# First mixer's attention tiles between the parts of the mLSTM heads, a norm per head, and the second mixer's probabilities in PSUM

## The reference

```python
# first block
h = rms_norm(x, g); z = h @ w_in
y_a = mlstm_group(q_m, k_m, v_m, o_m, gates, ...)   # 4 heads, both directions, 4 chunks of 128
y_b = mla_group(c_q, c_kv, k_pe, ...)               # 4 heads: softmax(q k^T) v over 512 keys
x = x + concat(y_a, y_b) @ w_out
h = rms_norm(x, g); x = x + square(relu(h @ w_ff1)) @ w_ff2
# second block
ret_out = silu(rg) * rmsnorm(retention(rq, rk, rv))
a = softmax(s0) - lam * softmax(s1)                 # causal, 4 heads
diff_out = rmsnorm(a @ v, g)
x = x + concat(ret_out, diff_out) @ w_out
x = x + peer(rmsnorm(x, g), ...)                    # 16 of 128 keys per half query, 16 of 256 pairs
out = rmsnorm(x, g)
# inside mlstm_group
h = rms_norm(h_fw + h_bw, g_out)                    # per head of 128 columns
return sigmoid(o) * h
```

## Time and profile before

| | |
|---|---|
| median of 3 runs | 2564.78 us (2561.06 to 2567.64) |
| profiled execution | 2563.88 us, its span 2562.1 us |
| busy in the span | PE 94%, DVE 52%, ACT 31%, POOL 33% |
| first mixer, four mLSTM heads | 164.9 to 261.2 us |
| first mixer, 16 attention tiles | 261.3 to 327.6 us |
| second mixer, differential tiles | about 815 to 932 us |
| wait for the last key selection | 1139.9 to 1150.0 us |

### The profile page before, as it was taken

How to read it: one execution, slowest core, us unless ns; L and a number is a source line. 1 busy time by engine, 2 the same in 40 slices (tenths; PEclk the granted TensorE clock), 3 DMA queues, 4 the chain that set the end, 5 groups by cost and what they waited for, 6 DMA issues and landing times.

```text
span 2562.1 us, 29145 instructions
## 1 busy us (share of the span) xinstructions
PE 2404.5 (94%) x11589; PEld 1209.4 (47%) x11797; DVE 1329.6 (52%) x2379; ACT 805.9 (31%) x880; POOL 847.1 (33%) x221
## 2 busy tenths in 40 slices
PE   7987889999989888889999999999999999999998
PEld 3456445444444454444466544444444444444443
DVE  2654526454532542689999555555555552222223
ACT  3221324333332333211189532222222232323222
POOL 0000215555553144531000253333333333424231
PEclk9985899999999999999999999999999999999999
DMA  5010035988863105763467986666666657666531
GB/s 202 33 66 1 1 148 164 246 246 244 247 191 105 66 34 169 215 176 119 160 273 303 345 241 188 184 182 185 184 186 180 182 176 201 170 174 180 138 91 41
DMA packets 401649, 424.98 MB, mean 166 GB/s; under 512 B 275578, under 2 KB 342270, under 8 KB 388740
## 3 DMA queue, kind: packets, MB, share of 16 engines
q1 hardware_dynamic: 395204, 411.93, 53.2%
q10 hardware_dynamic: 6336, 11.54, 1.2%
HBM read 283.97 MB, written 72.35 MB: 139 GB/s over the span
## 4 chain that ended last, share of the span: by engine, by line
PE 74%; DVE 17%; ACT 4%; DMA 2%; issue 2%; POOL 1%; DVEq 0%; SPq 0%; POOLq 0%; ACTq 0%
PE ps L1490 43%; PE ps L1765 14%; DVE arena L2428 5%; DVE arena L2435 4%; PE ps L1803 2%; DMA gate_matrix<-split 2%; PE ps L1303 2%; ACT split L1224 2%; PE ps L1588 1%; ACT arena L1210 1%; PE ps L1301 1%; PE ps L1276 1%; PE ps L1781 1%; PE ps L1432 1%; PE ps L1782 1%
## 5 line engine op out<-in xcount | busy, mean ns | idle before, releaser
L1490 PE MATMUL ps<-split,arena 128*128 128x512 bf16 x4232 | 936.6, 380 | 22.8 <-DVE x_sb L2450 9.0
L1490 PEld LDWEIGHTS ps<-split,arena 128*128 128x128 bf16 x4320 | 421.2, 98 | 534.1 <-DVE x_sb L2450 14.4
L852 POOL TENSOR_TENSOR split<-ring,split 128x4096 bf16<-128x4096 f32 x32 | 259.3, 8103 | 892.1 <-ACT split L1224 892.1
L1765 PE MATMUL ps<-arena 128*128 128x512 bf16 x1881 | 415.4, 379 | 2.1
L2450 DVE TENSOR_TENSOR x_sb<-ps,x_sb 128x512 f32<-128x512 f32 x256 | 173.8, 689 | 323.2 <-PE ps L1490 323.2
L759 POOL TENSOR_TENSOR split<-ring,split 128x4096 bf16<-128x4096 f32 x27 | 215.2, 7970 | 293.3 <-ACT split L1001 266.5
L1490 PE MATMUL ps<-arena,split 128*128 128x512 bf16 x1314 | 293.8, 381 | 13.1 <-DVE arena L2156 6.6
L2428 DVE TENSOR_TENSOR arena<-arena 128x512 f32<-128x512 f32 x128 | 179.7, 1404 | 238.4 <-ACT arena L1217 142.1
L1765 PEld LDWEIGHTS ps<-arena 128*128 128x128 bf16 x1920 | 187.9, 98 | 226.5
L1490 PEld LDWEIGHTS ps<-arena,split 128*128 128x128 bf16 x1344 | 142.7, 107 | 158.4 <-issue 9.8
L2435 DVE TENSOR_TENSOR arena<-arena 128x512 bf16<-128x512 f32 x128 | 157.2, 1228 | 67.4 <-ACT arena L1210 33.7
(11 more groups left out here) (300 smaller groups left out, 2457.6 us busy)
## 6 DMA issues: line engine op xcount, KB each, us to landing
ring<-in_peer_v SPq DMA_DIRECT2D x32, 2048.0 KB, 7.7
ring<-in_peer_u SPq DMA_DIRECT2D x20, 2048.0 KB, 8.3
ring<-in_w_ff SPq DMA_DIRECT2D x16, 2048.0 KB, 8.3
gate_matrix<-split SPq DMA_DIRECT2D x16, 2048.0 KB, 8.2
arena<-gate_matrix SPq DMA_DIRECT2D x32, 1024.0 KB, 8.4
arena<-in_peer_u SPq DMA_DIRECT2D x48, 512.0 KB, 4.7
turned_table<-u_split SPq DMA_DIRECT2D x48, 512.0 KB, 5.4
ring<-turned_table SPq DMA_DIRECT2D x12, 2048.0 KB, 9.5
```

The source lines that it names most:

```text
L852: pool.tensor_tensor(split[:, s2, 1, :], ring[:, slot, :], split[:, s2, 0, :], ALU.subtract).then_inc(w_lo, 1)
L1490: mm = pe.matmul(dst, a(k), b(k), start=n == 0, stop=n == len(terms) - 1)
L1765: mm = pe.matmul(up_bank(j), a, b, start=n == 0, stop=n == len(terms) - 1)
```

## The change

1. The attention tiles move in between the parts of the mLSTM heads, on PE, DVE and ACT. Head h carries tiles 4h to 4h + 3. Bank 1 holds the scores, bank 6 the transposed tile, bank 7 the result, one each instead of two by turns; the states' updates go to banks 4 and 5, the one-column products to bank 0.
2. The norm is taken per head: POOL makes four factors at a time, DVE multiplies head h's four blocks during head h + 1 (those of the last head after all tiles). The sigmoid stands first on ACT.
3. ACT rounds w_out's chunk 0 after head 2's squares, and chunk 1 after the last squares. POOL subtracts chunk 0 in four quarters between the norm factors of head 1 and head 2, chunk 1 after head 3's. Two rows of scratch change places to make room.
4. Second mixer: ACT writes the exponentials to the PSUM bank of the tile's scores; L2292 and L2294 read them there. `dif_score(i)` therefore waits for the probabilities of tile i - 2 instead of its maxima. DVE's copy L2261 moves behind the maxima.
5. PEER: of the 25 early tiles only tile 2 waits for the 15th selection and tile 3 for the 16th; tiles 0 and 1 don't wait.

PE:

```diff
+            def attend_score(i):
+                if i >= 1:
+                    pe.wait_ge(att_exp, i)
+                pe.matmul(bank(1), nopeT[...], nopeT[...], start=True, stop=False)
+                pe.matmul(bank(1), ropeT[...], ropeT[...], start=False, stop=True).then_inc(att_scores, 1)
+            def attend_turn(n):
+                pe.wait_ge(att_exp, n + 1)
+                if n >= 1:
+                    pe.wait_ge(att_out, n)
...
+            def attend_value(n):
+                pe.wait_ge(att_out, n + 1)
+                if n >= 1:
+                    pe.wait_ge(att_norm, n)
...
+            def attend(i):
+                attend_score(i)
+                if i >= 1:
+                    attend_turn(i - 1)
+                if i >= 2:
+                    attend_value(i - 2)
...
             for h in range(H):
+                if h >= 1:
+                    pe.wait_ge(head_read, h)
                 mlstm_scores(h)
+                attend(4 * h)
+                head_update(h)
+                attend(4 * h + 1)
+                head_values(h)
+                head_inter(h)
+                attend(4 * h + 2)
+                attend(4 * h + 3)
+            attend_turn(H * NT - 1)
+            attend_value(H * NT - 2)
+            attend_value(H * NT - 1)
```

`head_update`, `head_values` and `head_inter` are the old parts under names; `head_update(h)` also waits for `num_out` of head h - 1, and `head_values(h)` for `state_done`. DVE's order in a head (attend(i): maximum of tile i, copy of tile i - 1, division of tile i - 2):

```diff
+                # decayed keys, exponents' sum, then
+                attend(4 * h)
+                # states, probabilities, then
+                attend(4 * h + 1)
+                if h >= 1:
+                    head_rows(h - 1)
+                # sums with the states' part, then
+                attend(4 * h + 2)
+                # divisors, rows of y1, then
+                attend(4 * h + 3)
...
+            attend(H * NT)
+            attend(H * NT + 1)
+            head_rows(H - 1)
```

ACT and POOL:

```diff
                 act.activation(decay, decay, ACT.Exp).then_inc(decay_exp, 1)
+                attend_exp(4 * h)
+                attend_exp(4 * h + 1)
...
+                attend_exp(4 * h + 2)
+                attend_exp(4 * h + 3)
                 act.wait_ge(head_out, h + 1)
...
+                if h == 2:
+                    out_high(0)
+            squares.wait()
+            out_high(1)
...
-            inverse_rms(NT * H, DV, 3 * NT + NT * H)
+            mlstm_rms(0)
+            mlstm_rms(1)
+            pool.wait_ge(w_hi, 1)
+            for q in range(4):
+                cols = slice(q * 1024, (q + 1) * 1024)
+                first_low = pool.tensor_tensor(split[:, 0, 1, cols], ring[:, 1, cols], split[:, 0, 0, cols], ALU.subtract)
+            first_low.then_inc(w_lo, 1)
+            mlstm_rms(2)
+            mlstm_rms(3)
```

Second mixer and PEER:

```diff
-                    act.activation(dif[:, i % 2, m, 0:n_keys], dif[:, i % 2, m, 0:n_keys], ACT.Exp, ...
+                    act.activation(bank(4 * (i % 2) + m)[:, 0:n_keys], dif[:, i % 2, m, 0:n_keys], ACT.Exp, ...
...
-                    pe.wait_ge(dif_max, 2 * (i - 1))
+                    pe.wait_ge(dif_probs, i - 1)
...
-                    own.did(dve.tensor_scalar(dif[:, n % 2, 0, 0:n_keys], dif[:, n % 2, 0, 0:n_keys], row_inv[...], None, ALU.mult))
+                    own.did(dve.tensor_scalar(dif[:, n % 2, 0, 0:n_keys], bank(4 * (n % 2))[:, 0:n_keys], row_inv[...], None, ALU.mult))
...
-            pe.wait_ge(key_tops, 2 * P_HEADS)
             for m in range(SELECTED):
+                if m in (2, 3):
+                    pe.wait_ge(key_tops, 2 * P_HEADS - 3 + m)
```

More of the change, by code:

```diff
@@ L1096, in _ @@
                     act.wait_ge(dif_max, 2 * i + m + 1)
[L1097 removed]
+                    act.activation(bank(4 * (i % 2) + m)[:, 0:n_keys], dif[:, i % 2, m, 0:n_keys], ACT.Exp, bias=row_nmax[:, 2 * i + m:2 * i + m + 1],
                                    accum_out=row_sum[:, 2 * i + m:2 * i + m + 1]).then_inc(dif_exp, 1)
@@ new lines, in attend_score @@
+            def attend_score(i):
+                h, q = divmod(i, NT)
+                if i >= 1:
+                    pe.wait_ge(att_exp, i)
+                at = slice(h % 2 * A_ROPE, (h % 2 + 1) * A_ROPE)
+                pe.matmul(bank(1), nopeT[:, h, q * P:(q + 1) * P], nopeT[:, H + h, :], start=True, stop=False)
+                pe.matmul(bank(1), ropeT[at, h // 2, q * P:(q + 1) * P], ropeT[at, 2 + h // 2, :],
+                          start=False, stop=True).then_inc(att_scores, 1)
+            def attend_turn(n):
+                pe.wait_ge(att_exp, n + 1)
+                if n >= 1:
+                    pe.wait_ge(att_out, n)
+                for i in range(NT):
+                    mm = pe.transpose(bank(6)[:, i * P:(i + 1) * P], att[:, n % 2, i * P:(i + 1) * P], ident)
+                mm.then_inc(att_turned, 1)
@@ new lines, in attend_value @@
+            def attend_value(n):
+                pe.wait_ge(att_out, n + 1)
+                if n >= 1:
+                    pe.wait_ge(att_norm, n)
+                for i in range(NT):
+                    mm = pe.matmul(bank(7)[:, 0:DV], attT[:, n % 2, i * P:(i + 1) * P], v2[:, i, n // NT, :],
+                                   start=i == 0, stop=i == NT - 1)
+                mm.then_inc(att_pv, 1)
+            def attend(i):
+                attend_score(i)
+                if i >= 1:
+                    attend_turn(i - 1)
+                if i >= 2:
+                    attend_value(i - 2)
@@ L2037, in _, with attend, head_rows @@
             dve.wait_ge(ktok_done, 2)
+            def attend(i):
+                if i < H * NT:
+                    dve.wait_ge(att_scores, i + 1)
+                    own.did(dve.tensor_reduce(row_max[:, i:i + 1], bank(1), AX.X, ALU.max))
+                    own.wait()
+                    dve.tensor_scalar(row_nmax[:, i:i + 1], row_max[:, i:i + 1], -(A_DH ** -0.5), None, ALU.mult).then_inc(att_max, 1)
+                if 1 <= i <= H * NT:
+                    n = i - 1
+                    dve.wait_ge(att_turned, n + 1)
+                    if n >= 2:
+                        dve.wait_ge(att_pv, n - 1)
+                    dve.tensor_copy(attT[:, n % 2, :], bank(6)).then_inc(att_out, 1)
+                if i >= 2:
+                    n = i - 2
+                    h, q = divmod(n, NT)
+                    own.did(dve.reciprocal(row_inv[:, n:n + 1], row_sum[:, n:n + 1]))
+                    dve.wait_ge(att_pv, n + 1)
+                    own.wait()
+                    dve.tensor_scalar(y1[:, q, 512 + h * DV:512 + (h + 1) * DV], bank(7)[:, 0:DV],
+                                      row_inv[:, n:n + 1], None, ALU.mult).then_inc(att_norm, 1)
+            def head_rows(h):
+                dve.wait_ge(rstd_done, 3 + h)
+                v = slice(h * DV, (h + 1) * DV)
+                for t in range(NT):
+                    dve.scalar_tensor_tensor(y1[:, t, v], y1[:, t, v], rstd[:, h * NT + t:h * NT + t + 1], o1[:, t, v],
+                                             ALU.mult, ALU.mult).then_inc(y_ready, 1)
             for h in range(H):
```

155 lines of the change are left out of this document (53 added, 102 removed).

## The result

| | before | after |
|---|---|---|
| median | 2565.47 us (2561.06 to 2567.64, 4 runs) | 2497.39 us (2496.80 to 2498.01, 4 runs) |
| span of the profiled execution | 2562.1 us | 2495.0 us |
| PE busy, mean granted clock | 94%, 0.965 | 95%, 0.984 |

The ratio is 0.9737, with a 95% interval of 0.972 to 0.9754. The forecast was 2519, and the result lies 5.6 us under the lower end of the range. The sign was right, the size was not: 68 us where 45 were forecast.

What follows compares the result with a forecast made beforehand. PE was held back by idling at the lower clock in the first mixer and by waits for probabilities and the last selection; first mixer 40.8, second 3 and PEER 1.3 us off 2563.9 gave 2519 us, range 2503 to 2552.

Steps and rivals of the forecast that it cites:

- The loss of 0.5 us a tile: Differential tiles: balance of the scores' earlier wait against the moved DVE copy, 8 us lost in all (bounds 0 and 16).
- 9.1 - 8: Differential tiles: 9.1 us saved on DVE's instructions, less 8 us lost because the scores wait for the probabilities earlier.
- gives back about as much: Differential tiles: moving DVE's copy L2261 returns about what the scores' earlier wait costs, as DVE starts after the transposes.
- The instructions' saving of 9.1 us: Differential tiles: L2292 and L2294 shrink when reading PSUM, 16 x (0.12 + 0.45) us off a chain PE waits for.
- half of 6% of 117 us: Differential tiles: half of the clock losses in slots come back, taken as 2 us of PE work.
- the 6 us for lost clock in heads 1 to 3: First mixer: mLSTM scores in three later heads could lose the upper clock level, two thirds of 3.1 us each time.
- the 2.5 us for POOL's quarters: First mixer, head 3: POOL's 8 us of quarters hold head 2's norm factors, delaying DVE and its tiles (bounds 0 and 8).
- ACT's chunk: End of first mixer: ACT rounds chunk 1 (3.6 us) right before copying the first transposed features; 0.8 us sticks out.
- The gain of 1.3: PEER: tiles 0 and 1 fill the 10.1 us wait and DVE's copies start earlier, 1.3 us less (0 to 2).
- (a): First mixer: clock flips, each head's mLSTM work losing the upper level for half the head; 2541 us (2530 to 2555), chance 0.22.
- (b): First mixer: lower clock level throughout, no stretch long enough to raise it; slower, 2577 us (2570 to 2590), chance 0.10.
- (c): First mixer: DVE is the bound, its queue making a head 29 us at the upper level; 2534 us, chance 0.08.

Runs made afterwards that it cites:

- e1_mixer1: Kernel before with changes 1 to 3 only, second mixer and PEER as before: 2517.8 us, ratio 0.9815.
- e2_norm_late: Kernel after with all sixteen of DVE's norm multiplications behind the last attention tile: 2498.7 us.
- e2_shares: Kernel after with the w_in2 products dealt unevenly over the differential tiles' slots, more behind the widest scores: 2489.97 us.
- e2_no_peer: Kernel after without change 5, all 25 early tiles waiting for the 16th selection: 2496.54 us.
- e2_head0: Kernel after with PE's waits for the last keys and values moved behind the first head's mLSTM scores: 2483.86 us, ratio 0.9685.
- e1_order_only: Kernel before with PE's new slot order and DVE's copy behind the maxima, exponentials still in SBUF: 2554.14 us, ratio 0.9953.

## Why the prediction was wrong

**The failed step is change 4**: "`dif_score` of the next tile now waits for the same probabilities as `dif_turn`, and stands six bf16 products (1.46 us) plus itself earlier". That is the old order with the new wait. In the changed kernel ten products stand ahead of the scores, and the transposes follow them at once, so the probabilities are due later than before, not earlier. The loss of 0.5 us a tile does not exist. For the kernel that I had priced the total was right, 3 us (2561.79 against 2564.84, the interval being 0.3 to 5.4), but by luck in part: the stage gave 4.9 us, all of it from the clock (5.5 us less PE busy time, where I had 2) and none from the waits (0.8 us more, where 9.1 - 8 promised 1.1 less). The two large terms were there: the early wait cost 31.6 us alone, and moving the copy, which "gives back about as much", gave 36.5. Neither is a pure price. Of the 31.6 us 22.2 are waiting and 9.3 are PE work at a lower clock (103.2 us busy at PEclk 0.88). Three sizes were off besides. The instructions' saving of 9.1 us measured 6.8. I took L2294's to-be mean from L2269's 480 ns, and it is 551. And half of 6% of 117 us is 3.5 us, not 2.

In the kernel after, the waits fell by 12.8 us (19.0 to 6.2), where I had 1.1. With PSUM, it takes the order and the copy's place together: with one of them alone the waits are 18.0 or 19.8 us. PE's busy time fell by 6.7 us (93.9 to 87.2, at PEclk 1.00), where I had 2: when the long waits go, the whole clock loss comes back. These two are the missing 16.7 us, to 0.3.

**The first mixer** went by its mechanism. The fall came in the same place, the rise at 199 (forecast 198). Head 0 ended at 202.8 in an execution that began 1.8 us later, 0.5 us over the 200.5; heads 1 and 2 took 24.3 and 24.6 us (24), which with head 3 at the same rate is 1.4 us over; from there, 276.2, the tail takes 5.8 us (5). Two terms were too large: the 6 us for lost clock in heads 1 to 3 measured 0, as PEclk never left 1.00 between 200 and 282, and the 2.5 us for POOL's quarters measured 0 on PE. The quarters stood at 258.14 to 266.53 and DVE did wait 2.84 us for head 2's factors, but PE did not wait there. ACT's chunk was to cost 0.8 us and did not show either: it ends at 282.53, and the first copy starts at 282.80 behind a wait for PE. Together 9.3 us too many and 2.7 too few, which is the difference of 6.6 us. That head 0's level is a matter of chance was not foreseen: the stage takes 115.4, 106.3 or 102.2 us, so it can move this term by 13. All four executions of the kernel after, at 0.983 or 0.984, are on the long side.

**PEER.** The moved wait was forecast rightly, 8.2 + 0.6 us at L1837, and DVE's copies did start without the transposes. The gain of 1.3 was 0.84 on DVE, and the clock took 1.4 away on PE. I had written that "the clock is not lost before them" and had not asked whether it is lost behind them.

**The rivals.** (a), (b) and (c) are refuted by the same windows: PEclk 1.00 from 200 on, no wait for DVE over 1 us between 200 and 272. Beside (b) stood the rule of the Trainium skill, "TensorE: Matmul & The Clock Gate", section "Part 4: PE-mode transpose", that transposes don't count; the rise at 199 came right behind transposes and value products, as the trace of before had suggested, but it doesn't tell the two apart. The range failed because its lower end was built from bounds of a misread order: 10 us was the most that I gave change 4.

## What to carry to other kernels

Account for every hunk of a diff before pricing any: in a slot that two engines share, the order of the independent filler decides when a result is due; with the other two pieces in place it was worth 14.8 us, and the move to PSUM, which looked like the point, 7.9. Draw the loop from start to due time for the order as it will be; a piece that costs 31.6 us alone can gain 7.9 once the others are there. Where a stage begins with thin products, look for idle time that PE spends beside them on waits that they don't need: moving such waits, 1.4 us of idle time, took 13.5 us off the median here, since the level was then kept each time and not only sometimes.

## What was not expected of the hardware

- One kernel, two times, without any change: in e1_mixer1 four executions near 2518 us at a granted clock of 0.980 or 0.981, and one at 2506 with 0.986; the same split in e2_norm_late, e2_shares and e2_no_peer (the last: 2490 and 2491 at 0.988 and 0.987, 2497 to 2501 at 0.983 to 0.985). The kernels that kept the level in head 0 had none of it: eight executions within 2481.5 to 2485.1.
- Attention scores, half of them with 64 rows of contraction, and mLSTM scores with 64 and 36 rows hold the upper level when PE runs on (PEclk 1.00 over 102 us in e2_head0, with an idle time of 0.60 us in head 0). Whether such work brings it back varies: in the kernel before it did not from 261.3 to 269.3 (8 us busy without a break at 0.50), in the kernel after it took from 170 to 199, in e1_mixer1 it came at 177.7, in the scores of the second tile.
- One DVE instruction beside POOL's subtraction took up to 2.5 us instead of 0.75 (L2294, all operands in SBUF; in e1_order_only again 2.5). With one source in PSUM the longest was 0.75. Only this kernel's float32 work was seen.
